# The last residual add of a decoder trunk, done by accumulating DMAs into DRAM

## The reference, cut to what matters

```python
DEPTH, SEQ, D_MODEL = 2, 512, 1024      # float32 throughout
def rmsnorm(x, g):
    return x * rsqrt(mean(x * x, axis=-1) + 1e-6) * g

def reference(x, norm_gains, ...):
    for i in range(DEPTH):
        g = norm_gains[i]
        h = rmsnorm(x, g[0])
        m = retention_mixer(h, ...) if i % 2 == 0 else diff_attention_mixer(h, ...)
        x = x + rmsnorm(m, g[1])
        h = rmsnorm(x, g[2])
        x = x + rmsnorm((silu(h @ w_gate[i]) * (h @ w_up[i])) @ w_down[i], g[3])
    return x
```

## Time and profile before

| What | Value |
|---|---|
| time, median of 3 runs | 1403.31 us |
| the three runs | 1403.1, 1403.31 and 1406.35 us |
| span of the profiled execution (first to last instruction) | 1403.7 us |
| own time of the profiled execution beside its span | none recorded |
| PE, DVE, ACT, POOL busy | 98%, 41%, 32%, 6% of the span |
| last matrix product ends | 1396.5 us |
| DRAM read and written | 133.45 MB and 4.21 MB |

### The profile page before, as it was taken

One profiled execution on the slowest core, in us unless ns is written; L12 is line 12 of the kernel. 1 busy time (PEld: TensorE's weight loads), 2 busy tenths in 40 slices (PEclk: granted clock), 3 DMA queues, 4 the chain that ended last, 5 costly groups with the idle time before them and its releaser, 6 DMA issues.

```text
span 1403.7 us, 16624 instructions
## 1 busy us (share of the span) xinstructions
PE 1382.1 (98%) x6828; PEld 1160.3 (83%) x6828; DVE 574.3 (41%) x585; ACT 452.9 (32%) x536; POOL 80.1 (6%) x129
## 2 busy tenths in 40 slices
PE   7999999999999999999999999999999999999997
PEld 5888888888889888888888889899798888888886
DVE  4625344353344223222333656668552222223342
ACT  4233324233333222212222455466341221223231
POOL 1000000000011000000000212222110000000000
PEclk9999999999999999999999999999999999999999
DMA  6231323332222322233223122314122223332221
GB/s 236 91 108 61 108 86 112 120 120 87 94 87 86 98 90 90 90 119 120 90 90 135 31 77 96 97 45 150 60 91 90 90 90 99 104 111 90 90 90 60
DMA packets 90264, 136.09 MB, mean 97 GB/s; under 512 B 2635, under 2 KB 68427, under 8 KB 90228
## 3 DMA queue, kind: packets, MB, share of 16 engines
q1 hardware_dynamic: 88512, 132.06, 28.9%
q10 hardware_dynamic: 1716, 3.51, 0.7%
HBM read 133.45 MB, written 4.21 MB: 98 GB/s over the span
## 4 chain that ended last, share of the span: by engine, by line
PE 94%; DVE 3%; POOL 1%; ACT 1%; DMA 0%; issue 0%; POOLq 0%; DVEq 0%; SPq 0%; ACTq 0%
PE ps L1139 30%; PE ps L1141 30%; PE ps L1140 30%; PE ps L1370 1%; PE ps L1185 1%; POOL rstd L446 1%; PE ps L1391 1%; PE ps L1392 1%; PE ps L1299 0%; PE ps L1380 0%; DVE tmp L826 0%; DMA g_pre<-in_norm_gains 0%; DVE tmp L842 0%; POOL spare_lo L470 0%; ACT junk L530 0%
## 5 line engine op out<-in xcount | busy, mean ns | idle before, releaser
L808 DVE TENSOR_TENSOR w_lo<-raw,w_hi 128x2048 fp32r<-128x2048 f32 (+1 forms) x105 | 238.2, 2269 | 459.7 <-ACT w_hi L521 457.1
L1139 PE MATMUL ps<-h_hi,w_hi 128*128 128x512 f32 (+1 forms) x992 | 373.4, 376 | 0.0
L1141 PE MATMUL ps<-h_hi,w_lo 128*128 128x512 f32 (+1 forms) x992 | 372.6, 376 | 0.0
L1140 PE MATMUL ps<-h_lo,w_hi 128*128 128x512 f32 (+1 forms) x992 | 372.5, 375 | 0.0
L521 ACT ACTIVATE w_hi<-raw 128x2048 fp32r<-128x2048 f32 x103 | 197.0, 1913 | 376.4 <-PE ps L1141 375.3
L1139 PEld LDWEIGHTS ps<-h_hi,w_hi 128*128 128x128 f32 x992 | 186.7, 188 | 34.0 <-DVE w_lo L808 0.2
L1140 PEld LDWEIGHTS ps<-h_lo,w_hi 128*128 128x128 f32 x992 | 186.8, 188 | 33.7
L1141 PEld LDWEIGHTS ps<-h_hi,w_lo 128*128 128x128 f32 x992 | 186.7, 188 | 33.7
L1139 PE MATMUL ps<-w_hi,act_hi 128*128 128x512 f32 x448 | 178.0, 397 | 0.1
L1141 PE MATMUL ps<-w_hi,act_lo 128*128 128x512 f32 x448 | 177.6, 396 | 0.0
L1140 PE MATMUL ps<-w_lo,act_hi 128*128 128x512 f32 x448 | 177.5, 396 | 0.0
(11 more groups left out here) (156 smaller groups left out, 1469.6 us busy)
## 6 DMA issues: line engine op xcount, KB each, us to landing
raw<-in_ret_w_in SPq DMA_DIRECT2D x23, 1024.0 KB, 5.2
raw<-in_ffn_w_gate SPq DMA_DIRECT2D x22, 1024.0 KB, 5.4
raw<-in_ffn_w_up SPq DMA_DIRECT2D x22, 1024.0 KB, 5.4
raw<-in_ffn_w_down SPq DMA_DIRECT2D x22, 1024.0 KB, 4.9
raw<-in_ret_w_out SPq DMA_DIRECT2D x8, 1024.0 KB, 4.9
raw<-in_diff_w_in SPq DMA_DIRECT2D x8, 1024.0 KB, 5.6
raw<-in_diff_w_in SPq DMA_DIRECT2D x8, 512.0 KB, 4.8
raw<-in_diff_w_out SPq DMA_DIRECT2D x4, 1024.0 KB, 4.9
```

Of the source, the lines that this page charges most:

```text
L808: nc.vector.tensor_tensor(out_ap, whole, high.bitcast(F32), ALU.subtract).then_inc(done, 1)
L1139: nc.tensor.matmul(out_ap, a_hi, b_hi, start=start, stop=False)
L1140: nc.tensor.matmul(out_ap, a_hi, b_lo, start=False, stop=False)
L1141: return nc.tensor.matmul(out_ap, a_lo, b_hi, start=False, stop=stop)
```

## The change

The last addition is moved out of DVE. SP stores x as it stands after sub-layer 3 to `out`, four DMAs counted by a new semaphore `x_stored`, between the loads of the last gate-and-up products and those of the last `closing`. In the last boundary DVE scales each row tile from PSUM straight into x (whose old values are in `out` by then) instead of into `tmp`, and adds nothing; t = 3 is scaled in two halves. POOL then issues a DMA for each scaled piece that adds it to what is in `out` (`accum_op=ALU.add`). These DMAs stand in POOL's own queue between the four `post` steps. SP's five last stores are gone; it waits for the four early stores and the five accumulating ones.

```diff
@@ SP
             closing(2)
             gate_up(1)
+            sp.wait_ge(x_added, 3 * ST)
+            for t in range(ST):
+                sp.dma_start(out[0, t * P:(t + 1) * P, :], x[:, t, :]).then_inc(x_stored, 16)
             closing(3)
-            for t in range(ST - 1):
-                sp.wait_ge(x_added, 3 * ST + t + 1)
-                sp.dma_start(out[0, t * P:(t + 1) * P, :], x[:, t, :]).then_inc(out_done, 16)
-            for half in range(2):
-                cols = slice(half * D // 2, (half + 1) * D // 2)
-                sp.wait_ge(x_added, 4 * ST + half)
-                sp.dma_start(out[0, S - P:S, cols], x[:, ST - 1, cols]).then_inc(out_done, 16)
+            sp.wait_ge(x_stored, 16 * ST)
             sp.wait_ge(out_done, 16 * (ST + 1))
@@ POOL
+            def add_to_out(n, t, cols):
+                pool.wait_ge(post_scaled, 3 * ST + n + 1)
+                nc.gpsimd.dma_start(out[0, t * P:(t + 1) * P, cols], x[:, t, cols],
+                                    accum_op=ALU.add).then_inc(out_done, 16)
+
             def boundary(c):
+                if c == 3:
+                    pool.wait_ge(x_stored, 16 * ST)
+                    for t in range(ST):
+                        post(c, t)
+                        if t < ST - 1:
+                            add_to_out(t, t, slice(0, D))
+                    for half in range(2):
+                        add_to_out(ST - 1 + half, ST - 1, slice(half * D // 2, (half + 1) * D // 2))
+                    return
                 post(c, 0)
                 post(c, 1)
-                if c == 3:
-                    post(c, 2)
-                    post(c, 3)
-                    return
@@ DVE
+            def last_scale(t, halves):
+
+                dve.wait_ge(post_rstd, 3 * ST + t + 1)
+                if t == 0:
+                    dve.wait_ge(gpost_in, 16 * 4)
+                    dve.wait_ge(x_stored, 16 * ST)
+                n = D // halves
+                for cols in (slice(i * n, i * n + n) for i in range(halves)):
+                    nc.vector.scalar_tensor_tensor(out=x[:, t, cols], in0=bank(2 * t, 2)[:, cols],
+                                                   scalar=rstd[:, t:t + 1], in1=g_post[:, cols],
+                                                   op0=ALU.mult, op1=ALU.mult).then_inc(post_scaled, 1)
+
+            def boundary(c):
+                if c == 3:
+                    for t in range(ST):
+                        last_scale(t, 2 if t == ST - 1 else 1)
                     return
```

More of the change, by code:

```diff
@@ L181, in build @@
         out_done = sem("out_done")
+        x_stored = sem("x_stored")
         set_up = sem("set_up")
@@ L848, in post_add @@
                 dve.wait_ge(x_added, ST * c + t)
[L849 to L853, removed]
+                nc.vector.tensor_tensor(x[:, t, :], x[:, t, :], tmp[:, POST_PLACE[t], :], ALU.add).then_inc(x_added, 1)
+            def last_scale(t, halves):
[12 more added lines that the diff above has]
+                        last_scale(t, 2 if t == ST - 1 else 1)
                     return
-                nc.vector.tensor_tensor(x[:, t, :], x[:, t, :], tmp[:, POST_PLACE[t], :], ALU.add).then_inc(x_added, 1)
-            def boundary(c):
-                for t in range(2 if c < 3 else ST):
+                for t in range(2):
                     post_scale(c, t)
                     post_add(c, t)
-                if c == 3:
-                    return
                 nxt = CLOSERS[c][0] + CLOSERS[c][1]
```

## The result

The changed kernel takes 1407.89 us (median of 11 runs, 1405.27 to 1408.6), the kernel before 1403.54 us (median of 11 runs beside it, 1403.1 to 1406.35). The ratio is 1.002, 95% interval 1.0011 to 1.0028, so slower by 0.11% to 0.28%: less than the 0.3% called "no change" above, but not zero.

What follows compares the result with a forecast made beforehand. PE, busy 98% of the span, bounds the kernel, so mainly the tail behind its last product counts. DVE's 1.26 us gain against POOL's issues and landing, 2D + L - 3.95 = +1.85, gives 1405.2 us; range 1402.1 to 1408.7.

Steps and rivals of the forecast that it cites:

- D: Time one accumulating DMA holds POOL while being issued, behind the last product; taken as 1.1 us, bounds 0.33 and 2.42.
- the sum: Landing of the last piece behind the last product: 2D + L - 3.95 us against before, +1.85 us, time 1405.2 us.
- L: Time from the end of the second half's issue to its landing in `out`; taken as 3.6 us, bounds 1.8 and 4.5.
- the median of the runs lies 0.4 under the span: Step from profiled span to run time: span 1403.7 us, median 1403.31, so adding 1.85 gives 1405.2 us.
- Early stores: SP's four stores of x after the last up load: four issues of 0.36 us hidden in SP's idle time, cost 0.
- the sum's worst case: The last up load waits for all four early stores, 10.4 us later, landing at 1249.8; ACT wants it at 1251.38.
- GpSimd's queue: Tiles 0 to 2's DMAs between POOL's factors: tile 1's factor 0.5 us late, tiles 2 and 3 on time, cost 0.
- The small gain: Rival at the end: issue as short as SP's, read of `out` hidden; 1402.1 to 1403.2 us, typically 1402.6; chance 0.12.
- POOL's issue as the tail: Rival: the last two DMAs in POOL's queue cost 2D, deciding from D = 2.3 us; 1408.6 us at D = 2.8; chance 0.09.
- The slow accumulation: Rival: accumulating transfers slow, tile 2's 512 KB taking 10.1 us and tile 3's halves queueing behind; 1409.0 us; chance 0.09.
- GpSimd's turn from arithmetic to a DMA: Rival: POOL pays at each such turn; behind the last factor it passes 0.3% from 2.3 us; chance 0.03.
- PE was not starved: Rival denied here: early stores delay loads after 1234 by over 12 us, stopping PE at 1251; 1408.2 us at 3 us late; chance 0.01.

Runs made afterwards that it cites:

- run 3: Changed kernel with the scaled rows stored by SP and the last addition left out; ratio 0.9997 to the kernel before, tail behind the last matrix product 5.97 us.
- run 2: Changed kernel with GpSimd's DMAs storing without adding, so the last addition is left out; ratio 0.9996 to the kernel before, tail behind the last product 6.86 us.
- run 1: Kernel before plus the four early stores of x, its own last additions and stores kept; ratio 1.0001 to the kernel before.

## Why the prediction was right, point by point

The step that explains the result is the forecast's own: DVE gives 1.26 us back, and GpSimd's issue and the slower landing take more. By the runs the 1.93 us of tail split as

- **-1.26 us**, DVE's additions gone (run 3 against before: 5.97 against 7.23). Forecast 1.26.
- **+0.89 us**, GpSimd instead of SP for a plain store (run 2 against run 3: 6.86 against 5.97). From DVE's start to the end of the last issue it is 2.25 us instead of 1.77, the landing behind it takes 2.0 us instead of 1.7, and the program ends some 0.1 us later behind the landing (0.5 us instead of 0.4).
- **+2.30 us**, the addition in the DMA (the change against run 2: 9.16 against 6.86). 0.57 us of it is issue (0.88 us for a DMA instead of 0.60), 1.7 to 1.8 the landing.

Of the two unknowns, D was taken as 1.1 us and measured 0.88; what the sum lacked is the 0.29 us between DVE's end and GpSimd's start (0.05 assumed). Together they bring the end of the last issue to 1401.35 instead of 1401.55. L was taken as 3.6 us and measured about 3.8 (landing at 1405.1), and 0.5 us and not 0.4 follow it. So the mechanism was right and each of its sizes was off by 0.1 to 0.25 us; that +1.85 was forecast and +1.93 measured is partly luck, since D was too long and the other three too short. To place L near the upper bound was the right choice; its reason, a read and then a write of the whole piece, is not shown by it. The formula of the Trainium skill for GpSimd's DMAs ("DMA: Bandwidth & Descriptors", section "Anatomy of one DMA") makes 2.6 us for 256 KB, an estimate. The plain DMAs of run 2 bear it out, with 2.4 and 2.5 us from the start of the issue to the landing; the accumulating ones, with 3.6 and 4.9 us, do not.

**The absolute time** was off by 2.7 us (1405.2 forecast, 1407.89 measured) although the difference of the tails was right, and this step failed: "the median of the runs lies 0.4 under the span, so 1403.31 + 1.85". It takes one median for the kernel's time, where there are two levels. 1403.31 is a time of the lower one. On that level the forecast holds (1405.27 to 1405.73), but eight of the eleven runs of the changed kernel fell on the upper one. The span of 1403.7 belongs to the upper level already: in every kernel run here the time is 1.74 to 1.86 us above the span of the same run, so the profiled execution of before took about 1405.5 us. 1405.5 + 1.85 = 1407.35; the profiled run of the changed kernel took 1407.40. The range of 1402.1 to 1408.7 holds the measured median, but it has no term for the levels; it was wide enough for another reason, the unknown D and L.

**Early stores.** Cost 0, as forecast (run 1). The timeline of SP after, against the earlier trace rows:

```profile
1233.95 0.37 SPq L324 DMA_DIRECT2D raw<-in_ffn_w_up  x1
1234.53 2.34 SPq L428 DMA_DIRECT2D out<-x  x4
1245.73 0.40 SPq L324 DMA_DIRECT2D raw<-in_ffn_w_down  x1
```

Four issues took 2.34 us and not 1.4. The stores, which run beside each other and the load, landed 7.2 to 9.2 us after their issue, where one store alone takes 2.6 us. The last landed at about 1245.5, only 0.2 us ahead of SP's next load and later than four stores one after another would have by the sum (10.4 us). The load did not wait for them, as the sum's worst case had it: it landed in 6.5 instead of 5.4 us, 11 us ahead of its use:

```profile
1251.35 1.92 ACT L529 ACTIVATE w_hi<-raw 128x2048 fp32r<-128x2048 f32 x1 [7.97 <-PE ps L1157]
```

**GpSimd's queue.** The factor for tile 1 starts late, the ones for tiles 2 and 3 do not, as forecast (GpSimd's timeline, against the earlier trace rows):

```profile
1380.69 1.08 POOL L456 DMA_DIRECT2D out<-x  x1 [1.65 <-DVE x L867]
1381.46 0.54 POOL L442 TENSOR_TENSOR rstd<-ssq,eps 128x1 f32<-128x1 f32 x1
...
1392.15 0.18 POOL L442 TENSOR_TENSOR rstd<-ssq,eps 128x1 f32<-128x1 f32 x1 [6.98 <-ACT junk L538]
```

**The rivals.** The small gain fails on both D and L. POOL's issue as the tail would have needed D of 2.3 us. The slow accumulation exists, but in the size of the forecast: tile 2's 512 KB landed 5.5 us after issue and not 10.1. GpSimd's turn from arithmetic to a DMA shows nothing beyond the 0.29 us ahead of the DMA and 0.2 us once, for its first DMA. PE was not starved.

**The rule on additions.** The DMA engines' busy share for the same bytes is 1.0% with the addition and 0.4% without, 2.5 times. In the packet records of the two traces a packet of 4096 bytes of a 512 KB piece took 328 ns with the addition and 161 ns without (medians, the change and run 2), 2.0 times. The Trainium skill ("Collectives: The Full Stack", section "The bandwidth ceiling: the fold count and why AG ≠ RS ≠ AR") puts an addition at half the rate of a copy, because each piece is read from two places. This case's trace agrees for the single packet; in sum the engines were busy longer than the rule has it. The prediction's estimate by that page, 3.6 us of landing at most, was passed by 0.2 us. That the second read is the cause was not tried: no run separates it from the addition itself.

## What to carry to other kernels

An add behind the last product is a matter of the latency of a chain, not of an engine's load: taking 1.26 us of work from DVE helped only while the store that followed stayed as cheap. Price the whole chain to the landing: two plain stores from GpSimd cost 0.9 us more here than SP's two, and adding in them 2.3 us more. The price of adding grows with the bytes, and a finer cut does not lower it, because every piece is paid again in issue. Work that can be done before the last scalar is known (the gain of the norm) may be moved into the wait for it; that gave three quarters of the same saving, 0.95 us of tail, without a DMA of another kind. And compare a stage (here the tail) before comparing whole runs, when whole runs vary by more than the change.

## What the runs showed of the hardware

The two levels of whole runs appear in every kernel here, whatever its tail. In the windows of the profiles they differ where PE runs the small matrix products of the attention. Windows of the kernel before (upper level), with busy us of PE, PEld, DVE, ACT, POOL, then PE's granted clock:

```profile
810.00:820.00 10.00, 8.30 (x68) 7.87 (x69) 4.94 (x6) 5.91 (x8) 0.00 (x0) 0.94 0.45 148
820.00:830.00 10.00, 10.00 (x80) 9.78 (x79) 7.41 (x21) 8.12 (x19) 2.20 (x3) 0.89 0.29 89
```

The same windows of run 1 (lower level):

```profile
810.00:820.00 10.00, 8.30 (x76) 7.87 (x75) 5.09 (x8) 6.54 (x8) 0.00 (x0) 1.00 0.55 174
820.00:830.00 10.00, 10.00 (x85) 10.00 (x85) 8.87 (x21) 7.39 (x19) 4.07 (x4) 1.00 0.21 63
```

PE was idle for 1.7 us in 810 to 820 in both; in one the granted clock fell for part of the 20 us (means 0.94 and 0.89, so for a while the lower level of 1.2 GHz for 2.4), in the other it stayed at 1.00, and the last product came 2.1 us earlier. 0.06 and 0.11 of 10 us each are 1.7 us of full clock lost at this spot; the other 0.4 us are not placed. Why the same program gets one or the other is open. With 3 of 11 against 6 of 11 runs on the lower level, the changed kernel may fall on the upper one more often or by chance. For chance speaks that the spot lies 400 us ahead of the first instruction that the change touches, and that the count varies as much without an accumulating DMA: 7 of 11 runs on the lower level in run 2, 2 of 11 in run 3.
